# Last projections of two layers begun with the k-tiles that are complete, gating beside them, and rows squared tile by tile

## The reference

```python
# layer 0: mix = [A 512 | B 512 | M 256]
A = silu(gate_a) * chunked_sgu(gelu(u), gelu(v))
B = silu(gate_b) * (1 - lam_init) * rms_norm(diff_attention(...), subln)    # per head of 64
M = silu(gate_m) * memory_attention(...)
x = x + concat([A, B, M]) @ l0_w_out                                        # (512, 1280) @ (1280, 1024)
h = rms_norm(x, l1_norm)
# layer 1: mix = [C 512 | D 512 | M 256]
C = silu(gate_c) * silu(rms_norm(conv(...), c_norm))
D = silu(gate_d) * nsa(...)
M = silu(gate_m) * memory_attention(...)
x = x + concat([C, D, M]) @ l1_w_out
h = rms_norm_2(x, norm1_g) * (1 + scale) + shift                            # second block
```

## Time and profile before

| | |
|---|---|
| median of 3 runs | 3508.86 us (3505.54 to 3509.53) |
| the profiled execution's own time | 3507.94 us |
| its span | 3506.1 us |
| busy share of the span | PE 87%, DVE 36%, ACT 18%, POOL 7% |
| mean granted TensorE clock | 0.924 of full speed |

### The profile page before, as it was taken

One profiled execution on the slowest core, in us unless ns is written; L12 is line 12 of the kernel. 1 busy time (PEld: TensorE's weight loads), 2 busy tenths in 40 slices (PEclk: granted clock), 3 DMA queues, 4 the chain that ended last, 5 costly groups with the idle time before them and its releaser, 6 DMA issues. The chain is left out here.

```text
span 3506.1 us, 44346 instructions
## 1 busy us (share of the span) xinstructions
PE 3036.8 (87%) x18941; PEld 1800.3 (51%) x18941; DVE 1249.6 (36%) x2383; ACT 645.4 (18%) x1427; POOL 250.2 (7%) x347
## 2 busy tenths in 40 slices
PE   5899298899887859997999996979999978889888
PEld 2344275345576335555888884446544533334443
DVE  1000753158254039932556555364101221111111
ACT  2000332101243035412211211343100200000000
POOL 0000010000010000001333430020000000000000
PEclk8899679898897969998999998989999989999999
DMA  9421000323000411100000003120422159999998
GB/s 312 147 72 54 15 1 16 90 83 87 0 1 1 142 61 48 48 11 27 3 2 2 3 2 116 42 97 1 160 87 72 71 221 413 413 413 413 413 413 351
DMA packets 161244, 431.73 MB, mean 123 GB/s; under 512 B 33006, under 2 KB 44530, under 8 KB 159893
## 3 DMA queue, kind: packets, MB, share of 16 engines
q1 hardware_dynamic: 161050, 428.90, 32.5%
HBM read 418.22 MB, written 10.66 MB: 122 GB/s over the span
## 5 line engine op out<-in xcount | busy, mean ns | idle before, releaser
L328 PE MATMUL banks<-weight_ring,rows_turned 128*128 128x512 f32 (+1 forms) x1064 | 451.0, 584 | 38.8 <-DMA weight_ring<-in_w_in 30.0
L328 PEld LDWEIGHTS banks<-weight_ring,rows_turned 128*128 128x128 f32 x1064 | 200.4, 196 | 284.9 <-issue 280.2
L2123 PE MATMUL banks<-rows_turned,weight_ring 128*128 128x256 f32 (+1 forms) x768 | 252.5, 488 | 0.8 <-PEq L463 0.5
L252 PE MATMUL banks<-weight_ring,rows_turned 128*128 128x512 f32 x512 | 221.6, 593 | 3.0 <-PE banks L252 1.8
L2123 PEld LDWEIGHTS banks<-rows_turned,weight_ring 128*128 128x128 f32 x768 | 146.9, 192 | 99.7 <-issue 84.9
L3335 PE MATMUL banks<-weight_ring,chosen_turned 128*64 128x512 f32 (+1 forms) x696 | 176.7, 561 | 16.9 <-DMA weight_ring<-in_w_up 10.9
L3335 PE MATMUL banks<-expert_weights_early,chosen_turned 128*64 128x512 f32 (+1 forms) x672 | 171.5, 564 | 11.7 <-DMA expert_weights_early<-in_w_up 9.0
L252 PEld LDWEIGHTS banks<-weight_ring,rows_turned 128*128 128x128 f32 x512 | 96.6, 190 | 128.0 <-issue 128.0
L252 PE MATMUL banks<-weight_ring,mix_turned 128*128 128x512 f32 x320 | 140.6, 601 | 8.4 <-DMA weight_ring<-in_l_w_out 7.2
L3436 DVE TENSOR_TENSOR hidden<-hidden,banks 128x512 f32<-128x512 f32 (+1 forms) x24 | 14.0, 638 | 338.6 <-PE banks L3335 338.6
L2358 PE MATMUL banks<-v_channels 64*64 64x64 f32 (+1 forms) x2880 | 119.5, 229 | 0.7
(11 more groups left out here) (551 smaller groups left out, 4639.4 us busy)
## 6 DMA issues: line engine op xcount, KB each, us to landing
weight_ring<-in_w_gate SPq DMA_DIRECT2D x29, 1408.0 KB, 17.9
weight_ring<-in_w_up SPq DMA_DIRECT2D x29, 1408.0 KB, 16.8
expert_weights_early<-in_w_gate SPq DMA_DIRECT2D x28, 1408.0 KB, 19.7
expert_weights_early<-in_w_up SPq DMA_DIRECT2D x28, 1408.0 KB, 17.9
expert_weights_early<-in_w_down SPq DMA_DIRECT2D x36, 1024.0 KB, 17.7
weight_ring<-in_w_down SPq DMA_DIRECT2D x35, 1024.0 KB, 19.0
weight_ring<-in_l_w_in SPq DMA_DIRECT2D x15, 2048.0 KB, 8.4
weight_ring<-in_w_in SPq DMA_DIRECT2D x13, 2048.0 KB, 7.8
```

What stands on the lines that cost most here:

```text
L252: ins = nc.tensor.matmul(kit.ps[0:m, u % 8, 0:cols], lhsT, rhs, start=(k0 + j == 0), stop=(k0 + j == matrix.nk - 1))
L328: ins = kit.nc.tensor.matmul(self.bank(u), lhsT, rhs, start=(k == 0), stop=(k == nk - 1))
L2123: ins = nc.tensor.matmul(kit.ps[:, bank(u), 0:n], w[:, k, f * P:(f + 1) * P], hT[:, k, h0:h0 + n], start=(k == 0), stop=(k == KD - 1))
```

## The change

The gating, the turning and the projection of each layer become one block, `project_mix`, which is used by both layers.

- TensorE turns the six complete k-tiles first (layer 0: 0 to 3, 8, 9; layer 1: 4 to 9), multiplies them for the first group of columns, waits for the gating (`late_ready`), turns the other four k-tiles, finishes the first group and goes through the second. The chunks of `w_out` are now 4, 2 and 4 k-tiles for each group, in that order; they were 5 and 5.
- ScalarE alone copies the turned k-tiles, out of two banks (6 and 7); the products use the other six. It makes the six early copies, its part of the gating, then the four late copies.
- VectorE does its part of the gating, then the additions.
- SyncE requests the projection's weights from the beginning of this block.
- When VectorE has added the last group of a token tile, ScalarE squares that tile, and after four it takes the root into `row_roots`. The norm behind (`roots=row_roots`) leaves squares and root out and begins with the reciprocal.

The core of the diff:

```diff
-    m["out0"] = Matrix(stream, a["l0_w_out"], columns(0, D), 5)
+    m["out0"] = Matrix(stream, a["l0_w_out"], columns(0, D), k_parts=[(0, 4), (8, 2), (4, 4)])
...
-    m["out1"] = Matrix(stream, a["l1_w_out"], columns(0, D), 5)
+    m["out1"] = Matrix(stream, a["l1_w_out"], columns(0, D), k_parts=[(4, 4), (8, 2), (0, 4)])
...
+def project_mix(kit, stream, matrix, x, mix, mixT, early, roots, vector, scalar):
...
+    ks = early + [k for k in range(NK) if k not in early]
+    NE = len(early)
+    R = 6
...
+        def bank(i):
+            return kit.ps[:, R + i % 2, :].rearrange("p (t n) -> p t n", t=TX)
...
+            def turn(i):
+                if i >= 2:
+                    pe.wait_ge(kept.sem, kept(i - 1))
+                for t in range(TX):
+                    ins = nc.tensor.transpose(bank(i)[:, t, :], mix[:, t, ks[i] * P:(ks[i] + 1) * P], kit.ident)
+                ins.then_inc(turned.sem, 1)
+            for i in range(NE):
+                turn(i)
+            for g, (n0, nn, chunks) in enumerate(matrix.groups):
+                done = 0
+                for c, (i, k0, kk) in enumerate(chunks):
+                    if g == 0 and done == NE:
+                        pe.wait_ge(late_ready.sem, late_ready(1))
+                        for j in range(NE, NK):
+                            turn(j)
+                    done += kk
+                    if g == 0:
+                        pe.wait_ge(kept.sem, kept(done))
+                    stream.arrived(pe, i)
+                    w = stream.chunk(i)
+                    for t in range(TX):
+                        u = TX * g + t
+                        if c == 0 and u >= R:
+                            pe.wait_ge(taken.sem, taken(u - R + 1))
+                        for j in range(kk):
+                            ins = nc.tensor.matmul(kit.ps[:, u % R, 0:nn], mixT[:, k0 + j, t * P:(t + 1) * P], w[:, j, :],
+                                                   start=(c == 0 and j == 0), stop=(done == NK and j == kk - 1))
...
+        def act_program(act):
+            def keep(i):
+                act.wait_ge(turned.sem, turned(i + 1))
+                nc.scalar.activation(mixT[:, ks[i], :].rearrange("p (t n) -> p t n", t=TX), bank(i), ACT.Copy).then_inc(kept.sem, 1)
+            for i in range(NE):
+                keep(i)
+            scalar(act)
+            for i in range(NE, NK):
+                keep(i)
+            for t in range(TX):
+                act.wait_ge(taken.sem, taken(total - TX + t + 1))
+                if t:
+                    act.wait_ge(sums.sem, sums(t))
+                nc.scalar.activation(junk[:, :], x[:, t, :], ACT.Square, scale=D ** -0.5, accum_out=roots[:, t:t + 1]).then_inc(sums.sem, 1)
+            act.wait_ge(sums.sem, sums(TX))
+            kit.act_step(act, root(kit, roots[:, :]))
...
+        def dve_program(dve):
+            vector(dve)
+            dve.sem_inc(late_ready.sem, 1)
+            for g, (n0, nn, _) in enumerate(matrix.groups):
+                for t in range(TX):
+                    u = TX * g + t
+                    dve.wait_ge(products.sem, products(u + 1))
+                    dst = x[:, t, n0:n0 + nn]
+                    nc.vector.tensor_tensor(dst, dst, kit.ps[:, u % R, 0:nn], ALU.add).then_inc(taken.sem, 1)
+
+        def sync(sp):
+            stream.load_ahead(sp, matrix.last + 1)
...
-            elementwise(kit, vector=gate_vector, scalar=gate_root)
-        with ExitStack() as es:
             mixT = kit.sb(es, "mix_turned", [P, 10, SEQ])
-            turn_mix(kit, y[:, :, 0:1280], mixT)
-            project(kit, stream, m["out0"], residual_units(kit, x, mixT), engines=1)
+            project_mix(kit, stream, m["out0"], x, y[:, :, 0:1280], mixT, [0, 1, 2, 3, 8, 9], row_roots, gate_vector, gate_root)
...
+            project_mix(kit, stream, m["out1"], x, tb[:, :, 0:1280], mixT, [4, 5, 6, 7, 8, 9], row_roots, gate_vector, gate_scalar)
```

More of the change, by code:

```diff
@@ L205, in __init__ @@
         self.groups = []
+        if k_parts is None:
+            k_parts = columns(0, nk, k_step)
         for n0, nn in col_groups:
             chunks = []
-            for k0 in range(0, nk, k_step):
-                kk = min(k_step, nk - k0)
+            for k0, kk in k_parts:
                 chunks.append((stream.add(w[k0 * P:(k0 + kk) * P, n0:n0 + nn], kk, nn), k0, kk))
@@ L365, in by_tokens, with norm_and_turn @@
     return units
-def norm_and_turn(kit, src, tiles, dst, gain, shift=None, rows=None, sync=None, landed=None):
+def norm_and_turn(kit, src, tiles, dst, gain, shift=None, rows=None, sync=None, landed=None, roots=None):
     nc = kit.nc
@@ L411, in _ @@
             def _(act):
-                for i, t in enumerate(tiles):
+                for i, t in enumerate(tiles if roots is None else ()):
                     if i >= 1:
@@ L415, in _ @@
                     nc.scalar.activation(sq[:, :], src[:, t, :], ACT.Square, scale=src.shape[2] ** -0.5, accum_out=ss[:, i:i + 1]).then_inc(sums.sem, 1)
-                act.wait_ge(sums.sem, sums(T))
-                root(kit, ss[:, 0:T]).then_inc(rooted.sem, 1)
+                if roots is None:
+                    act.wait_ge(sums.sem, sums(T))
+                    root(kit, ss[:, 0:T]).then_inc(rooted.sem, 1)
                 for i in range(T):
@@ L1281, in elementwise @@
             block.sync(sync)
-def residual_units(kit, x, turned):
-    def units(n0, nn):
-        def unit(t):
-            def operands(w, j, k):
-                return turned[:, k, t * P:(t + 1) * P], w[:, j, :]
-            def put(eng, act, psum):
-                dst = x[:, t, n0:n0 + nn]
-                return kit.nc.vector.tensor_tensor(dst, dst, psum, ALU.add)
-            return P, nn, operands, put
-        return [unit(t) for t in range(TX)]
-    return units
 def turn_mix(kit, mix, turned):
@@ L1905, in load_early @@
                     sp.wait_ge(loaded.sem, loaded(16 * (len(pairs) - 1)))
-                norm_and_turn(kit, x, list(range(TX)), hT, g_in, sync=load_early, landed=(gain_landed.sem, gain_landed(16)))
+                norm_and_turn(kit, x, list(range(TX)), hT, g_in, sync=load_early, landed=(gain_landed.sem, gain_landed(16)), roots=row_roots)
                 second_rows(kit, hs, stream, m, hT, memT, dict(
@@ L1962, in second_layer, with gate_vector, gate_scalar @@
-        with ExitStack() as es:
-            mixT = kit.sb(es, "mix_turned", [P, 10, SEQ])
-            turn_mix(kit, tb[:, :, 0:1280], mixT)
-            project(kit, stream, m["out1"], residual_units(kit, x, mixT), engines=1)
+        normed = kit.counter("conv_normed", TX)
+        activated = kit.counter("conv_activated", TX)
+        with ExitStack() as e2:
+            sq = kit.sb(e2, "squares", [P, 1024])
+            ms = kit.sb(e2, "mean_squares", [P, TX])
+            sums = kit.counter("mean_squares_ready", 1)
+            roots = kit.counter("roots_ready", 1)
+            parts = [(yc[:, t, :].unsqueeze(1), yc[:, t, :].unsqueeze(1), cn[:, :]) for t in range(TX)]
+            def gate_vector(dve):
+                mean_squares(kit, dve, sq, ms, parts)
+                dve.sem_inc(sums.sem, 1)
+                dve.wait_ge(roots.sem, roots(1))
+                scale_rows(kit, dve, ms, parts)
+                dve.sem_inc(normed.sem, TX)
+                for t in range(TX):
+                    dve.wait_ge(activated.sem, activated(t + 1))
+                    step(dve, nc.vector.tensor_tensor(tb[:, t, CG:CG + 512], tb[:, t, CG:CG + 512], yc[:, t, :], ALU.mult))
+            def gate_scalar(act):
+                act.wait_ge(sums.sem, sums(1))
+                root(kit, ms[:, :]).then_inc(roots.sem, 1)
+                for t in range(TX):
+                    act.wait_ge(normed.sem, normed(t + 1))
+                    nc.scalar.activation(yc[:, t, :], yc[:, t, :], ACT.Silu).then_inc(activated.sem, 1)
+            mixT = kit.sb(e2, "mix_turned", [P, 10, SEQ])
+            project_mix(kit, stream, m["out1"], x, tb[:, :, 0:1280], mixT, [4, 5, 6, 7, 8, 9], row_roots, gate_vector, gate_scalar)
@@ L2008, in _, with second_block @@
             sp.wait_ge(parked.sem, parked(16 * len(pairs)))
-def second_block(kit, stream, m, a, x, out, place, place3, cols, rows_park):
+def second_block(kit, stream, m, a, x, out, place, place3, cols, rows_park, row_roots):
     nc = kit.nc
```

69 lines of the change are left out of this document (34 added, 35 removed).

## The result

The changed kernel takes 3450.1 us (median of 4 runs, 3449.11 to 3457.41) against 3507.2 (median of 4, 3503.09 to 3509.53) for the kernel before beside it: a ratio of 0.9843, 95% interval 0.9828 to 0.9858, or 57 us less. The forecast was 37 us less.

A forecast was written before the change was run, and what follows sets the result against it. TensorE, by far the busiest engine, was taken to stand still at the ends of layers 0 and 1. Projections -12.1 and -20.6, norms +1.3 and -5.7, sum to -37.1 us: from 3508.86 to 3472, range 3464 to 3480.

The forecast's parts named there:

- The overlap: Both projections: gating runs beside the first 48 matmul records, about 23 us, ending 12 us before TensorE asks.
- rival 4: Both projections: late half asked for before gating is done, TensorE waits some 3 to 6 us per layer: 3480; chance 0.035.
- First start of the matmuls: Both projections: matmuls begin 4.0 us after the block's start in layer 0, 5.8 in layer 1, there set by weights.
- The cold start: First matmuls of each projection: they begin at a lowered clock, costing 2.35 us in each layer.
- The pause: First column group of each projection: the four late transpose groups and copies take about 3.5 us before the last 16 matmuls.
- rival 1: Both projections: the clock falls again during the late transposes, costing 2.35 us in each layer: 3476; chance 0.20.
- The squares: Norms behind the projections: earlier squares and root cost 1.3 us behind layer 0 and gain 5.7 behind layer 1.
- SyncE's row: Small loads issued behind layer 0's projection: the later block start pushes them out, costing 1.3 us (bounds 0 and 1.6).
- The shift of the last projection in layer 1: End of layer 1's projection: its last matmul was to come 33 us earlier than before.
- the drain: ScalarE's table load before layer 1's root: about 1.38 us extra per change of set by the skill; the trace showed none.
- Rival 2: Both layers: warm matmul start in layer 0 and small loads paced by the chunk, 3468; shorter pauses reach 3464; chance 0.17.
- a change elsewhere, where the work is the same: Rest of the program: given 0 us in the sum; any change there was listed as a sign of being wrong.

The follow-up runs named there:

- a_gate_first: The changed kernel with TensorE waiting for the gating's end before its first transpose, and ScalarE gating ahead of its copies: 3481.39 us, ratio 0.9919.
- b_early_request: The kernel before, with only layer 1's projection weights requested earlier, at the beginning of the gating's block: 3501.37 us, ratio 0.9978.
- a_squares_back: The changed kernel with squares and root back in the norm behind each projection, new projection order and addresses kept: 3451.47 us, ratio 0.9832.

## Why the prediction was partly right

**The overlap: right.** The gate ran beside the first matmuls with 10 us to spare (12 forecast), TensorE never waited for it, and the projection's own work stayed at 34.6 to 34.7 us for each group of columns. Taking the overlap away (a_gate_first) costs its worth, 15.4 and 13.9 us. One slip changes nothing here: the cover is not the 23 us that the prediction sets against the gating (rival 4 too), but that and the first start, 27 in layer 0, as its own "until about 582" has it; measured are 24.2 and 26.7.

**First start of the matmuls: right within 0.4.** 3.63 against 4.0 in layer 0, 6.04 against 5.8 in layer 1. There the cause was the named one, the weights: 5.95 from request to landing. The cold transposes, 0.9 per group, were done 0.70 before the matmuls.

**The cold start: a term that was mis-sized in both blocks.** I counted 2.35 in each and it was 0 in each. In layer 0 the transposes follow TensorE's last work within 0.8 us, so the clock did not fall. In layer 1 it was low, and the transposes brought it back. I had taken the 0.52 from 1146 on for what matmuls meet behind transposes; b_early_request shows that it was what they meet behind 7 us of standing still. Two stretches of before, shown above beside that run, would have told me.

**The pause: 3.12, not 3.5,** and the clock stayed at 1.00 in it, so rival 1 did not happen. Here the Trainium skill's advice (Perfetto Trace Analysis, Matmul Optimizations) to keep matmuls back to back did not bite: the pause took its 3.12 us and no clock.

The blocks' errors sum up: in layer 0 2.35 (cold start) + 0.4 (first start) + 0.4 (pause), in layer 1 2.35 + 0.4 - 0.2, which is 3.1 and 2.5; the differences to the forecast are 3.1 and 2.4.

**The squares: right.** -6.1 against -5.7 in layer 1; the load did not land later after the last matmul than allowed; its two small loads took 1.72 to issue and not 4.90. In layer 0 +0.3 against +1.3. SyncE's row did start later (2.67 us after the last matmul, before 1.02), but its issue took 15.9 us and not 17.3. The shift of the last projection in layer 1 was given as 33 us, which leaves out the +1.3 of the same sum; it was 43.0. The root begins as the table load ends (1176.62 + 1.28, root at 1177.91): the drain that the Trainium skill gives (ScalarE: Activation LUTs, What ACT_TABLE_LOAD costs) does not show here either. Rival 2, everything kinder, comes nearest for the part at the change's own place: by 44.0 in place of 37.1 the time would have been 3465, inside the range.

**The step that failed** stands in the last sentence on what would prove me wrong: "or a change elsewhere, where the work is the same". The sum gave nothing to the rest of the program, and no reason for it; the rest gave 13.9 us. The new tile moved the addresses at which 5632- and 4096-byte descriptors land, and a stage whose DMA share is 1.02 for more than half a millisecond gained 11 to 12 us by it. That the change's own places gave 44.0 and not 37.1 would have kept the time inside the range; this did not. It is no part of the idea that was forecast, only of how its tile was allocated. I had followed the new tile's readers and writers, but not what is allocated behind it. Of the 13.9 us outside the change's places, 11.4 are this one (late part, 1610.5 to 1599.1); the other 2.5 have the size of the scatter.

**Open.** Why an aligned record stops at 215 ns (159 for 4096 bytes) was not settled, nor why only a quarter of the changed kernel's records are longer, and not the half that goes to the ring. Layer 1's unchanged part, 441.6 to 457.3 us, tends to be longer where the granted clock was lower; why it was granted less in one execution than in another was not shown.

## What to carry to other kernels

A change that adds or resizes an on-chip tile moves every tile allocated behind it; where a stage is bound by DMA, compare the landing addresses of its big rooms before and after, and test an edit of unused bytes by itself, before giving the gain to the logic. When costing a cold clock, read the clock just ahead of the matmuls and ask what TensorE did in the microseconds before: steady transposes had it back, a wait had lost it. Where a bracket names one releaser and the code waits for two things, compare the landing times with the copies, in a second run too. And when a computation leaves a handoff, look for the small loads that were beside it: moving those was worth another 16 us here.

## What the hardware showed that I had not expected

- The landing address in SBUF sets the speed of a transfer, with the same source and sizes: the experts' stage ran at 413 GB/s with the ring 192 and the experts' rooms 224 past a multiple of 256, at 420 with the ring 224 past and the rooms on one, and at 422 to 423 with all on one. From before that is 11.4 and 15.6 us. Between 50 and 100 us, where nearly all that lands is the ring's, 192 and 224 past gave 387 and 386 GB/s, a multiple of 256 gave 409.
- Matmuls behind transposes that follow each other closely start at a granted clock of 1.00, although those transposes began at 0.50 (1096.0 to 1100.0 in the changed kernel) or 0.54 on the mean (a_gate_first). In the pause of 3.1 us, where TensorE had 2.26 us of transposes in 3.20, it was 1.00.
- Fourteen small loads cost SyncE 15.9 to 17.3 us of issuing at a place where everything waits for them (630.98 to 646.86 in the changed kernel). With twelve of them beside the projection layer 0's block took 76.08 us, as without.
- Unchanged attention work in one layer took from 441.6 to 457.3 us in executions that otherwise agree within 1 us per block, with a mean granted clock of 0.88 to 0.92 over most of it. A gain of 6 us (a_squares_back) was visible in the stretches and not in the medians.
